# Two pieces of weights per chunk of input, the second three chunks behind, at the up projection and the gated linear unit

## The reference

```python
h = h + rmsnorm(mixed, norm_mix_post[i])
f = rmsnorm(h, norm_ffn_pre[i]) @ w_up[i]          # the up projection, 1024 -> 2 x 2816
f = causal_dwconv(f, conv_ffn[i]) + conv_ffn_b[i]
...
h = h + rmsnorm(e, norm_ple_post[i])               # the end of the first block
u = rms_norm(h, g)                                 # the second block's input
q, k, v, glu_a, glu_g = jnp.split(u @ w_in[l], splits, axis=-1)
u = a * jax.nn.sigmoid(g)                          # the gated linear unit
u = lax.conv_general_dilated(u, w_dw[:, None, :], ...)   # 31 taps, one channel at a time
```

## Time and profile before

| | |
|---|---|
| median of 3 runs | 1734.78 us (1734.14 to 1736.17) |
| the profiled execution's own time | 1732.11 us |
| its span | 1730.3 us |
| TensorE busy | 1620.4 us, 94% |
| VectorE, ScalarE, GpSimd busy | 922.6, 645.7, 143.9 us |
| mean granted TensorE clock | 0.957 of full speed |
| TensorE idle ahead of line 307, released by line 389 | 23.8 us, 13 times |
| TensorE idle ahead of line 307, released by line 294 | 10.5 us, 5 times |

### The profile page before, as it was taken

How to read it: one execution, slowest core, us unless ns; L and a number is a source line. 1 busy time by engine, 2 the same in 40 slices (tenths; PEclk the granted TensorE clock), 3 DMA queues, 4 the chain that set the end, 5 groups by cost and what they waited for, 6 DMA issues and landing times. The chain is left out here.

```text
span 1730.3 us, 20742 instructions
## 1 busy us (share of the span) xinstructions
PE 1620.4 (94%) x7966; PEld 1341.6 (78%) x7966; DVE 922.6 (53%) x1311; ACT 645.7 (37%) x905; POOL 143.9 (8%) x112
## 2 busy tenths in 40 slices
PE   7997998999999979999999979699999999999997
PEld 5786987978788867888888858477677788888886
DVE  5745447267544457777752254677764544444233
ACT  5343432145323234444432233355354444443211
POOL 0004301000000011000000000268110000000000
PEclk9988999899899999999999979899988999999998
DMA  5210005000032312322222313222011222222231
GB/s 197 73 62 1 1 6 197 19 19 2 20 108 91 122 49 73 114 95 94 95 75 100 99 58 110 75 88 83 25 31 67 74 98 96 97 97 77 99 100 66
DMA packets 22850, 131.96 MB, mean 76 GB/s; under 512 B 2604, under 2 KB 3116, under 8 KB 12924
## 3 DMA queue, kind: packets, MB, share of 16 engines
q1 hardware_dynamic: 21104, 123.54, 20.8%
q0 software_dynamic: 816, 6.15, 0.9%
q10 hardware_dynamic: 864, 1.36, 0.2%
HBM read 128.94 MB, written 2.10 MB: 76 GB/s over the span
## 5 line engine op out<-in xcount | busy, mean ns | idle before, releaser
L307 PE MATMUL ps<-AH,whi 128*128 128x512 f32 x1280 | 513.8, 401 | 61.6 <-DVE AL L389 23.8
L308 PE MATMUL ps<-AL,whi 128*128 128x512 f32 x1280 | 507.1, 396 | 0.0
L309 PE MATMUL ps<-AH,wlo 128*128 128x512 f32 x1280 | 506.7, 396 | 0.0
L294 DVE TENSOR_TENSOR wlo<-raw,whi 128x2048 fp32r<-128x2048 f32 (+4 forms) x126 | 252.8, 2006 | 274.9 <-ACT whi L287 274.5
L307 PEld LDWEIGHTS ps<-AH,whi 128*128 128x128 f32 x1280 | 245.5, 192 | 126.4 <-issue 27.4
L309 PEld LDWEIGHTS ps<-AH,wlo 128*128 128x128 f32 x1280 | 245.7, 192 | 52.6
L308 PEld LDWEIGHTS ps<-AL,whi 128*128 128x128 f32 x1280 | 246.3, 192 | 50.1
L287 ACT ACTIVATE whi<-raw 128x2048 fp32r<-128x2048 f32 (+4 forms) x126 | 210.6, 1671 | 161.1 <-PE ps L309 161.1
L307 PE MATMUL ps<-HH,whi 128*128 128x512 f32 x352 | 136.9, 389 | 0.0
L308 PE MATMUL ps<-HL,whi 128*128 128x512 f32 x352 | 136.9, 389 | 0.0
L309 PE MATMUL ps<-HH,wlo 128*128 128x512 f32 x352 | 136.9, 389 | 0.0
(11 more groups left out here) (352 smaller groups left out, 2092.6 us busy)
## 6 DMA issues: line engine op xcount, KB each, us to landing
raw<-wstream SPq DMA_DIRECT2D x74, 1024.0 KB, 4.8
raw<-wstream SPq DMA_DIRECT2D x32, 704.0 KB, 4.0
raw<-wstream SPq DMA_DIRECT2D x16, 768.0 KB, 4.2
raw<-wstream SPq DMA_DIRECT2D x8, 640.0 KB, 3.8
hT<-xT SPq DMA_DIRECT2D x4, 512.0 KB, 7.9
W1k<-w1k_d POOLq DMA_DIRECT2D x1, 2048.0 KB, 9.8
W1v<-w1v_d POOLq DMA_DIRECT2D x1, 2048.0 KB, 16.5
raw<-wstream SPq DMA_DIRECT2D x2, 512.0 KB, 3.4
```

The source lines that it names most:

```text
L294: nc.vector.tensor_tensor(WL[b][:, 0:n], RAW[b][:, 0:n], WH[b][:, 0:n].bitcast(F32), ALU.subtract).then_inc(w_lo_done, 1)
L307: nc.tensor.matmul(out_, WH[b][:, w], xh[:, k, :], start=start and k == 0, stop=False)
L308: nc.tensor.matmul(out_, WH[b][:, w], xl[:, k, :], start=False, stop=False)
L309: last = nc.tensor.matmul(out_, WL[b][:, w], xh[:, k, :], start=False, stop=stop and k == n - 1)
```

## The change

`two_pieces` replaces the entry loop at the up projection (`new` is 1) and at the gated linear unit (`new` is 3). In step n TensorE multiplies chunk n with both segments of piece 0, and from step 3 on also chunk n - 3 with both segments of piece 1. The column sums come in step 8, the spread in step 9, the last step is 10. At the up projection the start of piece 1 also waits for four chunks of the residual, since its banks hold results of the output projection which the residual reads; `ORDER[1]` brings chunks 5 and 6, which lie there, forward. To have piece 1 ready, its split moves ahead of the chunks: ScalarE's half ahead of the root, VectorE's between the reciprocal and the copy. The split of piece 2 moves out of the phase's loop to the same places at the next root. A Sqrt of one column at the start of `wo_act` is new; its result isn't used.

```diff
-        ORDER[1], ORDER[2] = (2, 3, 0, 1, 4, 5, 6, 7), (5, 6, 3, 4, 0, 1, 2, 7)
+        ORDER[1], ORDER[2] = (2, 3, 5, 6, 0, 1, 4, 7), (5, 6, 3, 4, 0, 1, 2, 7)
...
-        def rms_rest(dve, k, eps=EPS):
+        def rms_rest(dve, k, eps=EPS, between=None):
...
             nc.vector.reciprocal(RC[:, :], RC[:, :]).then_inc(rc_ready, 1)
+            if between:
+                between()
             dve.wait_ge(rows_ps, k + 1)
...
             if new is None:
                 return pairs(pe, ph, body)
+            if new in (1, 3):
+                two_pieces(pe, ph, new, norm)
+                return pairs(pe, ph, body, 1)
...
+        LAG = 3
+
+        def two_pieces(pe, ph, new, norm):
+
+            weights_ready(pe, ph, 0, 0)
+            bank_ready(pe, ph, 1)
+            for n in range(DC + LAG):
+                if n < DC:
+                    k = ORDER[new][n]
+                    pe.wait_ge(in_lo, 8 * new + n + 1)
+                    for s in range(2):
+                        ins = product(ps[:, ring(ph, s), :], 0, 8 * s + k, 1, AH[:, k:k + 1, :], AL[:, k:k + 1, :],
+                                      start=n == 0, stop=n == DC - 1)
+                        if n == DC - 1:
+                            ins.then_inc(seg_done, 1)
+                if n == LAG:
+                    weights_ready(pe, ph, 0, 1)
+                    bank_ready(pe, ph, 3)
+                    if ph == "up":
+                        pe.wait_ge(h_ready, 4)
+                if n >= LAG:
+                    k = ORDER[new][n - LAG]
+                    for s in range(2):
+                        ins = product(ps[:, ring(ph, 2 + s), :], 1, 8 * s + k, 1, AH[:, k:k + 1, :], AL[:, k:k + 1, :],
+                                      start=n == LAG, stop=n == DC + LAG - 1)
+                        if n == DC + LAG - 1:
+                            ins.then_inc(seg_done, 1)
+                if n == DC:
+                    add_gathered(pe, norm, total=TOTAL[norm])
+                if n == DC + LAG - 2:
+                    spread_rms(pe, norm)
...
         def wo_act(act):
+            nc.scalar.activation(col("lneps"), col("eps"), ACT.Sqrt)
...
         def up_act(act):
...
-                    if early:
+                    if early and b:
                         stage_hi(act, "up", i, b, last)
...
         def up_dve(dve):
...
-                    if early:
+                    if early and b:
                         stage_lo(dve, "up", i, b, last)
...
-                stage_hi(act, "glu", i, b, i == 1)
+                if c:
+                    stage_hi(act, "glu", i, b, i == 1)
                 products(5)
...
-                stage_lo(dve, "glu", i, b, i == 1)
                 if c:
+                    stage_lo(dve, "glu", i, b, i == 1)
                     dve.wait_ge(ug_ready, c + 1)
                     taps(EARLY)
...
             wo_act(act)
+            stage_hi(act, "wo", 1, 1, True)
             rms_root(act, 1)
             normed_input_act(act, 1, 2, "ffn_pre", 0)
-            stage_hi(act, "wo", 1, 1, True)
+            stage_hi(act, "up", 0, 0, False)
             rms_root(act, 2)
...
             ple_act(act)
+            stage_hi(act, "ple", 3, 1, True)
             rms_root(act, 4)
-            stage_hi(act, "ple", 3, 1, True)
             normed_input_act(act, 3, 5, "mix2", 16)
+            stage_hi(act, "glu", 0, 0, False)
             rms_root(act, 5)
...
-            rms_rest(dve, 1)
+            rms_rest(dve, 1, between=lambda: stage_lo(dve, "wo", 1, 1, True))
...
-            stage_lo(dve, "wo", 1, 1, True)
-            rms_rest(dve, 2)
+            rms_rest(dve, 2, between=lambda: stage_lo(dve, "up", 0, 0, False))
...
-            rms_rest(dve, 4, eps=4 * EPS)
+            rms_rest(dve, 4, eps=4 * EPS, between=lambda: stage_lo(dve, "ple", 3, 1, True))
...
-            stage_lo(dve, "ple", 3, 1, True)
-            rms_rest(dve, 5)
+            rms_rest(dve, 5, between=lambda: stage_lo(dve, "glu", 0, 0, False))
```

## The result

| | before | after |
|---|---|---|
| median of 4 runs | 1735.47 us (1734.14 to 1736.51) | 1758.18 us (1755.46 to 1759.92) |
| ratio | | 1.013 (1.0112 to 1.0147) |
| the profiled execution's own time, span | 1732.11, 1730.3 us | 1758.42, 1756.6 us |
| TensorE busy | 1620.4 us | 1649.9 us |
| mean granted clock | 0.957 | 0.939 |

The forecast was 1732.8 us, between 1729.3 and 1736.3. Executions of these kernels fall in two groups, one from about 1726 to 1738 us and one from 1755 to 1767, and an execution of the second group is called **low** here; all 4 of the changed kernel are low, none of these 4 of the kernel before.

A forecast was written before the change was run, and what follows sets the result against it. TensorE is busy nearly the whole span, so only its idle or half-clock moments can be won, mostly waits for VectorE's input halves. Up -1.45 and GLU -0.5 sum to -1.95 from 1734.78: 1732.8 us, range 1729.3 to 1736.3.

The forecast's parts named there:

- The up loop (steps 1 to 4): Up projection: moved splits, column sums at 662.3, first scaling of results 1.45 us earlier, new order costs 0; term -1.45 us.
- The GLU (5 to 7): GLU: table load delays the root 1.07 us, first scaling 1.1 later, 0.7 regained in the convolution; term -0.5 us.
- rival D: Ahead of the GLU's root: the table load drains 1.38 us more, on the path to 1182.39; 1734.2 us, chance 0.08.
- The sum: Up's -1.45 and the GLU's -0.5 give -1.95 us, taken from the median 1734.78: 1732.8 us.
- Rival B: TensorE's own gain stays in up (3.1) and GLU (5.7, plus 2.8 clock): 1723.2 us, 0.07; half case 1730.2, 0.11.
- The clock: TensorE's restarts after waits, such as 1182.39: 14 matmuls at low clock cost 2.8 us; 1.5 us allowed to each side.
- Rival C: Chunks 3 to 8 of both doubled loops meet the low clock: 5.6 - 1.95 = +3.7 us, 1738.4; chance 0.05.
- Wrong: ... the granted clock below 1 within chunks 3 to 8: Sign against the forecast: TensorE's granted clock under 1 during chunks 3 to 8 of the changed loops; no size given.

The follow-up runs named there:

- run 10: The changed kernel with eleven unused matmuls in the value projection, 2.5 us, ahead of the attention: 1732.59 us, ratio 0.9996, 0 of 10 low.
- run 11: The changed kernel with four unused matmuls in the value projection, 0.9 us, ahead of the attention: 1734.23 us, ratio 0.9999, 3 of 10 low.
- run 1: The changed kernel with nine unused matmuls in the first down projection, 2.05 us: 1732.88 us, 2 of 8 low, the others at ratio 0.9978.
- run 8: The changed kernel with five unused matmuls filling only the attention's second idle time: 1729.71 us, ratio 0.9974, 0 of 12 low.
- run 9: The kernel before with four unused matmuls in the value projection, 0.9 us, ahead of the attention: 1737.69 us, ratio 1.0038, 4 of 10 low.
- run 12: The kernel before with eleven unused matmuls in the value projection, 2.5 us, ahead of the attention: 1736.96 us, ratio 1.0009, 0 of 10 low.
- run 6: The kernel before with both idle times at the attention's start filled by four and five unused matmuls: 1735.92 us, ratio 1.0008, 0 of 12 low.
- run 4: The changed kernel with both idle times at the attention's start filled by four and five unused matmuls: 1730.06 us, ratio 0.9971, 0 of 6 low.
- run 2: The changed kernel with the GLU put back as before, only the up projection changed: 1733.88 us, ratio 0.9983, 1 of 8 low.
- run 3: The changed kernel with the up projection put back as before, only the GLU changed: 1732.19 us, ratio 0.9985, 1 of 8 low.
- run 5: The changed kernel once more, unaltered: 1759.03 us, ratio 1.0147, 4 of 4 low.
- run 7: The changed kernel with the attention's second idle time made longer by two ScalarE copies: 1764.12 us, ratio 1.0169, 5 of 5 low.
- run 13: The changed kernel with four unused matmuls filling only the attention's first idle time: 1759.49 us, 3 of 4 low.

## Why the prediction was wrong

By its own steps:

- **The up loop** (steps 1 to 4): right in every start, and 1.78 us won instead of 1.45.
- **The GLU** (5 to 7): right. At the first scores it is worth 1.97 + 0.51 - 1.78 = 0.70 instead of 0.5. The load starts as the split ends (1084.71 + 1.89), its price is 1.28, and the root's activation follows 1.29 after its start; the drain that the Trainium skill adds (rival D) is not there.
- **The sum** of -1.95: the first scores start 1.97 us earlier, and 2.48 with the 0.51 by which the execution ran late; 0.33 of what that is above the forecast is up's and 0.2 the GLU's. Where the clock stays up, the whole time agrees in the direction. With the added work taken off, run 10 makes the change worth 0.7 + 2.5 = 3.2 us (1.6 to 4.9), run 11 0.2 + 0.9 = 1.1 (-1.2 to 3.3), run 1 3.8 + 2.05 = 5.9 (3.6 to 8.1); run 8 gives 4.5 (2.4 to 6.4). Three of the four lie above the forecast, two of them clear of it; what the 1 to 4 us more are was not looked for. Rival B is refuted: TensorE's gain became the wait of 6.44.
- **The clock** is the step that failed: "With several such starts shifted against each other I give 1.5 us to each side". It counted only the restarts after long waits for weights, at 14 slow matmuls each. It held the clock to be worth 1.5 us to each side. Shown instead is a fall of the clock behind an idle time of 1.26 us, in a stage that the prediction never read, and a low stretch of 65 us (1232 to 1297): 27.6 us, ten times the 2.8 of a restart.
- **Rival C** named the right kind of cause, the low clock, in the wrong place (inside the doubled loops, where the clock is 1.00 from chunk 3 to the column sums, 647.56 to 662.7 and 1107 to 1120) and at 3.7 us. Its chance of 0.05 was all that stood on the slower side. "Wrong: ... the granted clock below 1 within chunks 3 to 8" did not come either; the sign stood some 110 us behind the second loop.

What could have been read beforehand: in the kernel before the clock falls within the same attention, towards its end (0.57 from 1280 to 1300, above), behind column sums of 128x1 matmuls, and its matmuls are thin and broken by two idle times. A shift of 2 us of such a stage is a question to the clock, and here the answer was worth tens of us. What could not: the kernel before is low in 7 of 89 executions and its profile is one of the others, so no view of it shows the 1760 us; nor does the place table exist without the later runs. A fair forecast would have kept the likeliest value and given the low group a chance of its own.

**Open.** Run 11 (43.4) and run 9 (44.1) are low 3 and 4 times in 10, and their profiles are of the others; where the attention stood in their low executions isn't known. Runs 9 and 12 have the same place by their profiles (44.1 and 44.0), and one is low 4 times in 10, the other never. Why the changed kernel lands at the bad place each time, while the others scatter, isn't settled. Nor is what ends the low stretch: in the profile it ends in the middle of the mean's eight 512-column matmuls at 1291.88 (6.15 us for the eight, against 3.65 at full clock), the first dense ones in it, but no run moved them.

## What to carry over

When an edit shifts a later stage, read that stage's idle times and the width of its matmuls too, even if the edit doesn't touch it: here a gain of 2 us, forecast well at the attention's start, was lost more than ten times over behind one idle time of 1.26 us. If such a stage has a short idle time ahead of thin matmuls, fill it with a few dense matmuls into an unused bank; that cost nothing measurable (run 6) and left no low execution of the changed kernel in 18 (runs 4 and 8), which without it is low 8 times in 8. Judge by many executions and by the granted clock of each, since one profile shows one group only.

## What the runs showed of the hardware

- Once low, the clock stays low under the same work under which it stays high when it is high: TensorE is busy 46.00 of 46.00 us from 1234 to 1280 at 0.50 and likewise at 1.00. The groups of the attention's own matmuls (busy us, mean ns, idle before), before and after:

```profile
L1567 PE MATMUL ps<-KT,QT 64*128 64x512 f32 (+3 forms) x64 | 25.8, 507 | 0.8 <-DVE V L1783 0.8
L1585 PE MATMUL ps<-V,PT 128*128 128x64 f32 x160 | 23.4, 279 | 0.0
```

```profile
L1605 PE MATMUL ps<-KT,QT 64*128 64x512 f32 (+3 forms) x64 | 37.1, 694 | 0.8 <-DVE V L1822 0.8
L1623 PE MATMUL ps<-V,PT 128*128 128x64 f32 x160 | 34.6, 376 | 0.0
```

- The same page of the Trainium skill (Part 1) puts the penalty of the ramp, the slow matmuls ahead of a rise, under 1% of a typical kernel's span and advises against fitting to a count of them. What costs the time here is not a ramp but a fall inside the kernel with a long low stretch behind it, and one fall costs 1.5 to 1.7% (26.3 of 1730.3 us between the spans, 29.9 between those of the changed kernel and of run 8), so that figure can't be carried over to it.
- GpSimd's four additions take 6.72 us in every profile in which VectorE's split stands beside them (the kernel before, runs 2, 6, 9, 12) and 5.95 to 5.97 where it doesn't (the changed kernel, runs 1, 3, 4, 5, 7, 8, 10, 11, 13).
